# Query and key rows of a delta-rule layer left un-normalised, with their inverse lengths carried as factors per token

## The chip, the core and the metric

One core of a Trainium2 chip runs the whole program. The time is that of the device in microseconds (us), the median of three runs. The engines are TensorE (PE in the rows, its weight loads PEld), VectorE (DVE), ScalarE (ACT), GpSimd (POOL) and SyncE (SP), which here only issues DMAs.

## The reference, cut to what matters

The reference is two transformer blocks over 512 tokens of width 1024, in float32. The change lies in the second block, in its gated delta-rule branch:

```
qkv = silu(causal_conv(h @ w_qkv, conv_w))          # 4 taps, 3 x 1024 channels
q = l2_normalize(q) * DN_DK ** -0.5                  # per token and head, 8 heads of 128
k = l2_normalize(k)                                  # x * rsqrt(sum(x*x) + 1e-6)
beta = sigmoid(b);  g = -exp(a_log) * softplus(a + dt_bias)
o = chunk_gated_delta_rule(q, k, v, beta, g)
o = rms_norm(o, norm_g) * silu(z)
```

Within a chunk of 128 tokens the rule forms the matrix A[i,j] = beta_i * (k_i . k_j) * decay_ij below the diagonal, takes the inverse of (1 + A), applies it to beta * v and to beta * exp(g) * k, and updates a state of 128x128 per head. The rows of q enter the output only linearly, so a length left in them is a factor of the output row; the following root-mean-square norm has to know that factor because of its epsilon.

## The kernel before, in words

Each engine has its own instruction stream, written out in program order; semaphores couple the streams. Products go to eight PSUM banks in two rings of four: one ring is emptied by VectorE (`bank("dve")`, `take()` on VectorE), the other by ScalarE. An engine may run ahead of its partner by at most four banks.

The stage around the change, called the qkv stage here, comes after the sparse attention and before the delta rule. For two groups of four heads (g = 0, 1) and for the three parts q, k, v it makes four tiles of 128 channels by 512 tokens, 24 units in all. In a unit TensorE multiplies (eight matmuls of 128x512, each issued as two instructions, on the helper line 695), VectorE applies the four taps of the convolution out of the bank (L1884, L1889, then a one-element copy L1891 that frees the bank), and ScalarE applies silu in place (L2574).

Normalisation is interleaved. In each of the 16 units with part > 0, the tile made four units earlier (q while k is made, k while v is made) is normalised: VectorE squares it (L2075), TensorE multiplies it by a 128x128 matrix of ones so that each column holds the sum over the head's channels in all partitions (also L695), ScalarE takes the root (L2569) and signals with a small copy (L2571), VectorE takes the reciprocal over 128x512 (L2081) and multiplies the tile (L2082). VectorE's order in such a unit is: square, convolution, reciprocal, multiply; TensorE's order is: product of this unit, wait for the square, product with ones, product of the next unit.

After the 12 units of group 0, TensorE makes four row products for z (`z_rows`, L695 as well), emptied by ScalarE's silu (L2563). After group 1 it makes one, then `gains_along_rows` for both groups (16 instructions on L1173), which waits for VectorE's `gains_spread` (L2033). The stage thus holds 12 + 4 + 12 + 1 = 29 products of the same size and 16 products with ones.

Then come the chunks of the delta rule, `delta_step(g, ch, step)` with four chunks and 17 steps, the two groups alternating. On VectorE the odd steps below 14 update the inverse (L2131) and then do one part of the norm of the previous chunk's result (`result_norm`): part 1 is a reduction (L2054) and a multiply-add (L2055), part 2 a reciprocal of 128x4 (L2058). GpSimd masks and moves halves of the inverse (L2712, L2721). The inverse runs with five levels, on half-width matrices of 64 columns. Behind the last chunk, weight sums for the merge (L1765) wait for a weight transfer that SyncE starts after the last state update of the rule. `beg`, which is beta times exp(g), is made early, ahead of the index scores (L2005).

## Time and profile before

| | us |
|---|---|
| median of three runs (lowest, highest) | 2391.66 (2391.26, 2392.55) |
| the profiled execution, its own time | 2389.67 |
| its span, from the first to the last instruction | 2387.9 |
| TensorE busy | 2161.7 (91%) |
| VectorE busy | 1231.3 (52%) |
| ScalarE busy | 471.3 (20%) |
| qkv stage, from 1138.51 to 1361.66 of the span | 223.15 |

Rows give times from the start of the span. A timeline row has start, duration, engine, line, operation, output and input, and in brackets the idle time before it with what ended it. "x18" in a TensorE row is the number of merged instructions. The mean granted clock of TensorE is 0.955 of full speed in this execution.

### The profile page before, as it was taken

What the parts mean: (1) busy time and instruction counts of PE and PEld (TensorE: products, weight loads), DVE (VectorE), ACT (ScalarE), POOL (GpSimd) and SP (SyncE); (2) the same over time, 40 slices, a digit from 0 to 9 for tenths busy, and PEclk for the clock granted to TensorE, in tenths of its full rate; (3) what the DMA queues carried; (4) which work ended last, traced back from release to release, by engine and by line L of the source; (5) the groups of instructions that cost most, each with busy time, mean ns of one, the idle gap of its engine ahead of it and who ended that gap; (6) DMA issues with size and microseconds to landing.
All of it is one profiled execution on the core that took longest, in us unless ns stands there. A gap on an engine that the chain in (4) does not pass through costs nothing.

```text
span 2387.9 us, 23792 instructions
## 1 busy us (share of the span) xinstructions
PE 2161.7 (91%) x8806; PEld 1293.3 (54%) x8806; DVE 1231.3 (52%) x2129; ACT 471.3 (20%) x925; POOL 112.8 (5%) x143
## 2 busy tenths in 40 slices
PE   7998898999999999997999988899997799999873
PEld 3444344888888644434444466678864333333331
DVE  4684564666676522786575856677436321221113
ACT  1124441111000100125232433330001000000003
POOL 0000000000000000000000022210000010100000
PEclk9998898999999999899999999999998899999997
DMA  7126500522132212210111100021343799999994
GB/s 268 36 103 232 182 30 24 127 101 76 53 116 80 95 49 92 71 64 8 35 71 71 36 1 1 1 106 71 141 180 123 292 426 427 426 427 425 426 425 193
DMA packets 97289, 364.65 MB, mean 153 GB/s; under 512 B 10396, under 2 KB 19281, under 8 KB 84625
## 3 DMA queue, kind: packets, MB, share of 16 engines
q1 hardware_dynamic: 86337, 340.62, 36.9%
q0 software_dynamic: 8720, 20.89, 2.3%
q10 hardware_dynamic: 2112, 1.57, 0.2%
q8 instruction: 73, 1.20, 0.2%
q14 instruction: 47, 0.39, 0.0%
HBM read 357.00 MB, written 17.57 MB: 157 GB/s over the span
## 4 chain that ended last, share of the span: by engine, by line
PE 68%; DVE 16%; DMA 7%; ACT 4%; issue 4%; POOL 0%; SPq 0%; DVEq 0%; ACTq 0%; POOLq 0%
PE bank L695 45%; PE bank L1445 8%; PE bank L1440 5%; PE bank L760 2%; DVE mem L2081 2%; PE bank L1173 2%; PE bank L930 2%; DMA mem<-in_w_gate 2%; DMA mem<-in_w_down 2%; DMA mem<-in_w_up 2%; ACT mem L2405 1%; PE bank L805 1%; DVE mem L2022 1%; DVE mem L2021 1%; ACT L2569 1%
## 5 line engine op out<-in xcount | busy, mean ns | idle before, releaser
L695 PE MATMUL bank<-mem 128*128 128x256 f32 (+7 forms) x4688 | 1396.0, 459 | 39.8 <-ACT mem L2405 12.1
L695 PEld LDWEIGHTS bank<-mem 128*128 128x128 f32 (+1 forms) x4688 | 873.1, 193 | 512.1 <-issue 377.3
L1445 PE MATMUL bank<-mem 128*64 128x512 f32 x1248 | 283.5, 610 | 33.2 <-DMA mem<-in_w_up 13.4
L2405 ACT ACTIVATE mem<-bank 128x512 f32<-128x512 f32 (+6 forms) x262 | 133.9, 511 | 405.3 <-PE bank L695 159.6
L1445 PEld LDWEIGHTS bank<-mem 128*64 128x64 f32 x1248 | 93.5, 140 | 213.6 <-issue 201.2
L760 PE MATMUL bank<-mem 128*128 128x128 f32 (+1 forms) x692 | 118.8, 304 | 58.9 <-DVE mem L1679 24.2
L2341 DVE TENSOR_TENSOR mem<-mem,bank 128x512 f32<-128x512 f32 x19 | 13.1, 690 | 277.2 <-PE bank L1445 204.5
L760 PEld LDWEIGHTS bank<-mem 128*128 128x128 f32 (+1 forms) x692 | 85.1, 151 | 110.5 <-DVE mem L1679 37.2
L1440 PE MATMUL bank<-mem 128*128 128x512 f32 x288 | 128.9, 602 | 6.7 <-ACT mem L2665 4.1
L2518 ACT ACTIVATE mem<-bank 128x512 f32<-128x512 f32 (+1 forms) x50 | 29.1, 582 | 372.7 <-PE bank L695 371.0
L1440 PEld LDWEIGHTS bank<-mem 128*128 128x128 f32 x288 | 54.1, 191 | 76.6 <-issue 68.1
L2349 DVE TENSOR_TENSOR mem<-bank,mem 128x512 f32<-128x512 f32 x38 | 26.3, 693 | 106.6 <-PE bank L1445 73.9
L1173 PE MATMUL bank<-mem 128*128 128x128 f32 x512 | 69.0, 294 | 0.9 <-ACT mem L2405 0.8
L1173 PEld LDWEIGHTS bank<-mem 128*128 128x128 f32 x512 | 65.6, 208 | 3.5 <-ACT mem L2405 1.1
L2663 ACT ACTIVATE mem<-bank 128x512 f32<-128x512 f32 x19 | 11.4, 599 | 269.9 <-PE bank L1445 198.7
L2712 POOL TENSOR_TENSOR mem<-mem 128x256 f32<-128x256 f32 x40 | 36.9, 923 | 573.5 <-ACT mem L2405 561.2
L1765 DVE TENSOR_TENSOR mem<-mem 128x1024 f32<-128x1024 f32 (+2 forms) x25 | 29.1, 1163 | 56.1 <-PE bank L695 48.9
L2081 DVE RECIPROCAL mem<-mem 128x512 f32<-128x512 f32 x16 | 53.7, 3355 | 3.5 <-ACT mem L2571 3.5
L1889 DVE SCALAR_TENSOR_TENSOR mem<-bank,mem 128x511 f32<-128x511 f32 (+2 forms) x72 | 54.0, 750 | 2.6
L1884 DVE TENSOR_SCALAR mem<-bank,mem 128x512 f32<-128x512 f32 x24 | 18.0, 751 | 63.0 <-PE bank L695 62.5
L2665 ACT ACTIVATE mem<-bank 128x512 f32<-128x512 f32 x19 | 11.4, 599 | 172.0 <-PE bank L1461 172.0
L930 PE MATMUL bank<-mem 128*64 128x512 f32 (+7 forms) x128 | 41.7, 472 | 3.1 <-ACT mem L2405 3.1
(337 smaller groups left out, 1726.4 us busy)
## 6 DMA issues: line engine op xcount, KB each, us to landing
mem<-in_w_gate SPq DMA_DIRECT2D x37, 2048.0 KB, 25.2
mem<-in_w_up SPq DMA_DIRECT2D x37, 2048.0 KB, 24.4
mem<-in_w_down SPq DMA_DIRECT2D x36, 2048.0 KB, 26.0
mem<-in_w_in SPq DMA_DIRECT2D x18, 2048.0 KB, 7.7
mem<-in_w_ada SPq DMA_DIRECT2D x12, 2048.0 KB, 7.9
mem<-in_w_out SPq DMA_DIRECT2D x4, 2048.0 KB, 12.6
mem<-in_w_ple_gate SPq DMA_DIRECT2D x2, 2048.0 KB, 7.9
mem<-in_w_br_att SPq DMA_DIRECT2D x2, 2048.0 KB, 8.1
```

The costliest lines, as they stand in the source:

```text
L695: last = pe.matmul(o, l, r, start=(i == 0), stop=(i == len(pairs) - 1))
L760: last = pe.transpose(b[0:width, i * P:(i + 1) * P], s, ident)
L930: last = pe.matmul(o[:, k * P:SEQ], v_of(k, h), pT[:, h % nbuf, k, k * P:SEQ], start=(k == 0), stop=(k == NT - 1))
L1173: last = pe.matmul(b[:, h * P:(h + 1) * P], lhs(h), rhs(h), start=True, stop=True)
L1440: last_ = pe.matmul(o, lhs[:, k, :], ws[0][:, k, cols], start=(k == 0), stop=(k == kk - 1))
L1445: last_ = pe.matmul(o[here, :], lhs[:, k, here], w[:, k, cols], start=(k == 0), stop=(k == kk - 1))
L1765: V(tt(s1, feature_half(w, 0, 1), feature_half(w, 1, 1), ALU.add), w_summed)
L1889: V(stt(o, b[:, 0:SEQ - back], w_col(taps_ - 1 - back), o, ALU.mult, ALU.add), signal if back == taps_ - 1 else None)
L2081: V(dve.reciprocal(sq, sq))
L2405: C(act.activation(dst, src, ACT.Copy), act_free)
L2518: C(act.activation(dst[:, 0:cols], fast_bank(n, 3 * i)[:, 0:cols], ACT.Copy), fast_copied)
L2712: pool.tensor_tensor(B[f"L{lv % 2}"].rearrange("p h (a c) -> p h a c", a=half), level_order(B["AT"], lv)[:, :, half:2 * half, :], mask[:, ...
```

## The change

The query and key tiles stay as silu left them. ScalarE squares them instead of VectorE. TensorE sums the squares with four 128x128-by-one-column matmuls in place of one product with 512 columns, so that the sums stand per token in partitions, 4 columns per tile; VectorE adds epsilon and stores them in `lengths` (128 x 64 for q and k, 8 heads and 4 chunks). After the last unit one root on ScalarE and one reciprocal on VectorE serve all of them. The inverse length of k goes into beta: `beta_k` = beta/length scales v, and `beta` = beta/length squared scales A and, through `beg`, the keys. The inverse length of q times 128^-0.5 becomes a factor of the norm of the result (one multiply in part 1, one in part 2). The levels of the inverse are the same in both kernels; the diff holds no edit of them.

```diff
+        lengths = tiny(2 * NT * 8)
+        length_of = [lengths[:, j * NT * 8:(j + 1) * NT * 8].rearrange("p (a b) -> p a b", a=NT) for j in range(2)]
+        gain_of_q, gain_of_q2, beta_k = (tiny(NT * 8).rearrange("p (a b) -> p a b", a=NT) for _ in range(3))
...
 # TensorE, in each unit
                         if part:
-                            to_wait(to_pe)
-                            b = bank("act")
-                            full(product(b[:, :], [(const("ones"), flat(delta[0][("tmp", "decay")[i % 2]]))]), "act")
+                            to_wait(squares_ready)
+                            b = bank("dve")
+                            sq = flat(delta[0][("tmp", "decay")[i % 2]])
+                            for ch in range(NT):
+                                last = pe.matmul(b[:, ch:ch + 1], sq[:, ch * P:(ch + 1) * P], const("ones")[:, 0:1],
+                                                 start=True, stop=True)
+                            full(last, "dve")
+                            mark["squares", g, part, i] = done["dve"]
...
 # VectorE
-            V(tt(beg, beta, eg, ALU.mult))
...
                     V(dve.tensor_reduce(s, delta[g]["square"], AX.X, ALU.add))
+                    V(tt(s, s, gain_of_q2[:, ch, g * HG:(g + 1) * HG], ALU.mult))
                     V(ts(s, s, 1.0 / P, EPS, ALU.mult, ALU.add), square_summed[g])
                 if part == 2:
                     wait_next(square_rooted[g])
                     V(dve.reciprocal(s, s))
+                    V(tt(s, s, gain_of_q[:, ch, g * HG:(g + 1) * HG], ALU.mult))
...
-                        if part:
-                            before = S4["qkv"[part - 1]][:, g * HG + i, :]
-                            dve.wait_ge(silu_out, FT + 12 * g + 4 * (part - 1) + i + 1)
-                            sq = flat(delta[0][("tmp", "decay")[i % 2]])
-                            V(tt(sq, before, before, ALU.mult), to_pe)
                         m = part * 8 + g * 4 + i
                         conv(take(), S4[name][:, g * HG + i, :], CONV2,
                              lambda j: column("conv_w_2", j * 24 + m), None, silu_in)
                         if part:
-                            wait_next(from_act)
-                            V(dve.reciprocal(sq, sq))
-                            V(stt(before, before, DH ** -0.5 if part == 1 else 1.0, sq, ALU.mult, ALU.mult))
+                            V(ts(length_of[part - 1][:, :, g * HG + i], take()[:, 0:NT], EPS, None, ALU.add), dve_free)
+            V(dve.tensor_copy(stat8[:, 14:15], eps_col), lengths_summed)
             gains_spread(0, 0)
             gains_spread(1, 0)
+            wait_next(lengths_rooted)
+            V(dve.reciprocal(lengths, lengths))
+            V(ts(gain_of_q, length_of[0], DH ** -0.5, None, ALU.mult))
+            V(tt(gain_of_q2, gain_of_q, gain_of_q, ALU.mult))
+            V(tt(beta_k, beta, length_of[1], ALU.mult))
+            V(tt(beta, beta_k, length_of[1], ALU.mult))
+            V(tt(beg, beta, eg, ALU.mult))
...
-                    V(tt(B["v_b"], full_bank(), inner(beta[:, ch, gh], P), ALU.mult), dve_free)
+                    V(tt(B["v_b"], full_bank(), inner(beta_k[:, ch, gh], P), ALU.mult), dve_free)
...
 # ScalarE, in each unit
                         if part:
-                            C(act.activation(flat(delta[0][("tmp", "decay")[i % 2]]), take()[:, :], ACT.Sqrt,
-                                             bias=eps_col), act_free)
-                            C(act.activation(stat8[:, 15:16], eps_col, ACT.Copy), from_act)
+                            if i >= 2:
+                                act.wait_ge(dve_full, mark["squares", g, part, i - 2])
+                            elif part == 2:
+                                act.wait_ge(dve_full, mark["squares", g, 1, i + 2])
+                            C(act.activation(flat(delta[0][("tmp", "decay")[i % 2]]),
+                                             S4["qkv"[part - 1]][:, g * HG + i, :], ACT.Square), squares_ready)
                         wait_next(silu_in)
                         o = S4[name][:, g * HG + i, :]
                         C(act.activation(o, o, ACT.Silu), silu_out)
+                if g == 1:
+                    wait_next(lengths_summed)
+                    C(act.activation(lengths, lengths, ACT.Sqrt), lengths_rooted)
```

## Rows read from the trace of the kernel before

**Rows 1.** The first line of the page: the span.
```profile
span 2387.9 us, 23792 instructions
```
**Rows 2.** Chain of waits, 1120 to 1460: start, us, what.
```profile
1215.05 1.14 PE bank L695 x2
1216.25 1.28 ACT L2569
1218.57 3.37 DVE mem L2081
...
1231.83 63.06 PE bank L695 x146
```
**Rows 3.** Timeline of one unit with normalisation.
```profile
1215.05 8.01 PE L695 MATMUL bank<-mem 128*128 128x512 f32 x18 [0.39 <-DVE mem L2075]
...
1218.57 3.35 DVE L2081 RECIPROCAL mem<-mem 128x512 f32<-128x512 f32 x1 [0.25 <-ACT mem L2571]
...
1222.69 0.69 DVE L2075 TENSOR_TENSOR mem<-mem 128x512 f32<-128x512 f32 x1
...
1223.44 8.01 PE L695 MATMUL bank<-mem 128*128 128x512 f32 x18 [0.39 <-DVE mem L2075]
```
**Rows 4.** Windows, the qkv stage: us, busy and count by engine, granted clock.
```profile
1138.50:1361.60 223.10, 217.25 (x496) 92.59 (x496) 152.07 (x169) 74.17 (x93) 0.00 (x0) 1.00 0.16 57
```
**Rows 5.** Timeline, start of the stage and its end.
```profile
1138.51 42.40 PE L695 MATMUL bank<-mem 128*128 128x512 f32 x98 [0.85 <-DVE mem L2026]
...
1145.76 0.75 DVE L1884 TENSOR_SCALAR mem<-bank,mem 128x512 f32<-128x512 f32 x1 [7.31 <-PE bank L695]
...
1146.55 2.32 DVE L1889 SCALAR_TENSOR_TENSOR mem<-bank,mem 128x511 f32<-128x511 f32 x3
...
1152.64 0.75 DVE L1884 TENSOR_SCALAR mem<-bank,mem 128x512 f32<-128x512 f32 x1 [3.58 <-PE bank L695]
...
1361.66 2.05 PE L1173 MATMUL bank<-mem 128*128 128x128 f32 x16
```
**Rows 6.** Timeline of PE: other matmuls with few columns.
```profile
235.06 0.95 PE L819 MATMUL bank<-mem 128*128 128x1 f32 x8
...
969.85 0.95 PE L1135 MATMUL bank<-mem 128*128 128x8 f32 x8
```
**Rows 7.** Timeline of the delta rule around the norm of a result.
```profile
1444.25 0.86 POOL L2712 TENSOR_TENSOR mem<-mem 128x256 f32<-128x256 f32 x1
1444.57 0.56 DVE L2055 TENSOR_SCALAR mem<-mem 128x4 f32<-128x4 f32 x1
1445.16 0.42 DVE L2131 TENSOR_TENSOR mem<-mem,bank 128x256 f32<-128x256 f32 x1
...
1452.94 0.42 DVE L2131 TENSOR_TENSOR mem<-mem,bank 128x256 f32<-128x256 f32 x1 [2.31 <-PE bank L1284]
...
1454.76 0.17 DVE L2041 TENSOR_TENSOR mem<-mem 128x4 f32<-128x4 f32 x1
...
1587.91 0.17 DVE L2055 TENSOR_SCALAR mem<-mem 128x4 f32<-128x4 f32 x1
```
**Rows 8.** Timeline behind the last chunk.
```profile
1595.42 1.23 DVE L1765 TENSOR_TENSOR mem<-mem 128x1024 f32<-128x1024 f32 x1 [0.90 <-DMA mem<-in_w_br_att]
```
**Rows 9.** Timeline, small operations of VectorE ahead of the index scores.
```profile
973.01 0.19 DVE L2005 TENSOR_TENSOR mem<-mem 128x32 f32<-128x32 f32 x1 [1.70 <-ACT mem L2553]
```
**Rows 10.** Windows, a stretch of the delta rule with a lowered clock.
```profile
1410.00:1420.00 10.00, 7.13 (x50) 6.52 (x50) 2.22 (x4) 4.28 (x10) 0.00 (x0) 0.73 0.00 0
```
**Rows 11.** Timeline: the same product (eight instructions) at full and at lower clock.
```profile
1102.64 2.39 PE L930 MATMUL bank<-mem 128*128 128x512 f32 x8 [0.20 <-ACT mem L2405]
...
1133.05 4.60 PE L930 MATMUL bank<-mem 128*128 128x512 f32 x8 [0.84 <-ACT mem L2405]
```
**Rows 12.** Timeline of ACT: a square, then the table load of a root.
```profile
1791.02 1.15 ACT L2401 ACTIVATE mem<-mem 128x1024 f32<-128x1024 f32 x1
...
1792.28 1.28 ACT L2402 ACT_TABLE_LOAD   x1
```

More of the change, by code:

```diff
@@ L459, in build @@
         lower_moved = [sem(f"delta_lower_columns_moved{g}") for g in range(2)]
+        squares_ready, lengths_summed, lengths_rooted = (sem(f"qk_{n}") for n in ("squares_ready", "lengths_summed", "lengths_rooted"))
         square_summed, square_rooted, result_ready = ([sem(f"delta_{n}{g}") for g in range(2)]
```

## The prediction

> **What bounds the kernel now.** I read the chain of waits first, over the stage that the change touches. It alternates between two pictures. In the first five units and in the four z products it is TensorE alone, one product behind the other: the piece of 146 matmul instructions runs 63.06 us without a break [rows 2]. In a unit with normalisation it is a ring through three engines: two instructions of the product with ones on TensorE, a table load on ScalarE, the reciprocal of 3.37 us on VectorE [rows 2], then multiply, square, and TensorE again. The timeline says how long the ring is: TensorE starts the same group of 18 instructions at 1215.05 and at 1223.44, so a period is 8.39 us, and each time it has sat idle 0.39 us for VectorE's square [rows 3]. Without the ring a product takes 6.88 us, as the convolutions of two plain units start at 1145.76 and 1152.64 [rows 5]. So VectorE, at 8.39 us a unit, is the bound in this stretch, but TensorE is close behind it: the reader should see that an idle of 0.39 in 8.39 us is all that can be had there for taking VectorE away, plus what TensorE's own part of the normalisation shrinks. The window of the whole stage agrees: TensorE busy 217.25 of 223.10 us, at a granted clock of 1.00, VectorE 152.07 [rows 4].
>
> **The stage, new sum.** TensorE before: 29 products of 6.88 us are 199.5 us, 16 products with ones at two instructions of 0.43 us (6.88/16) are 13.8 us; together 213.3. The stage lasts 1361.66 - 1138.51 = 223.15 us [rows 5]. The other 9.8 us are idle time for VectorE and the refilling of the pipeline behind it: the first two instructions behind such a wait count 1.14 us in the chain instead of 0.86 [rows 2], and 0.39 + 0.28 = 0.67 in each of some 14 units is 9.4, which closes the account.
>
> After: four float32 matmuls of 128x128 by one column are eight instructions. The trace has the same shape elsewhere: eight on L819 in 0.95 us, and eight with 8 columns on L1135, again 0.95 us [rows 6]. The weight loads set this, not the columns. So the sums cost TensorE slightly more than before, 0.95 against 0.86 us, and a unit is 6.88 + 0.95 = 7.83 us if TensorE waits for nothing. Stage: 199.5 + 16 x 0.95 = 214.7 us, 8.4 us less than 223.15. Bounds: at 0.86 for a group the stage gains 10.0; if each group also pays the refill of 0.28 us seen behind a wait, 16 x 0.28 = 4.5 goes back and 3.9 is left. I take 8.4, since plain products follow each other at 6.88 us although each of them has a (satisfied) wait for a bank.
>
> The Trainium skill, TensorE: Matmul & The Clock Gate, section Back-to-back issue gap, gives about 81 ns for a sustained pair of weight load and matmul at 128 columns. By that the eight instructions would take 0.65 us and the stage would gain 13.2 us. The rows have 0.12 us each here (0.95/8), so the measurement speaks against that figure for float32 and I keep the row.
>
> Does TensorE wait? Take T as the end of a unit's product. VectorE convolves for 0.75 + 2.32 us and small change, until T + 3.3 [rows 5]. ScalarE then does silu and the square of the next unit, about 0.7 us each by the root's and square's size, until T + 4.8. TensorE wants that square at T + 7.83. There are 3 us of cover. A wait for the buffer two units back is long satisfied. VectorE now needs about 3.5 us a unit instead of 8.2: square, reciprocal and multiply are gone, 16 x (0.69 + 3.35 + 0.69) = 75.7 us of work, and all but the few us above were already beside TensorE. A small add of the sums (0.19 us, as L2005 [rows 9]) comes in their place, hidden. ScalarE loses 16 roots over 512 columns and both table loads per unit, 1.28 us each; they were in the ring, and go with it.
>
> **The end of the stage.** The new serial piece is: last sums, `lengths_summed`, root with a table load (1.28 + 0.25 us), reciprocal over 64 columns (3.35/512 x 64 = 0.42), five small operations of 0.19. From T of the last unit: VectorE at T + 3.9, the two `gains_spread` ahead of the wait, the root by T + 5.6, the rest by T + 7.1, two memsets (0.67 us) by T + 7.8. TensorE meanwhile has the sums and one z product in front of the gains: T + 7.83, and VectorE needs them 1 us later. So it is covered, by about 1 us; uncovered it would cost up to 1 us for every us it is longer. From the gains on, the order is as before. The load of silu's table for z moves to where ScalarE waits for the z product anyway. Cost 0, bounds 0 to 1.5.
>
> **The early edit.** L2005 leaves its place ahead of the index scores, where VectorE soon is the bound: -0.2 us [rows 9]; at the new place it is one of the five above. Bounds -0.2 to 0.
>
> **The delta rule.** 16 multiplies of 128x4 are added, two per result and group. The row nearest is L2041, the same operation and size, 0.17 us [rows 7], some 0.2 with its gap. Beside GpSimd's work a small operation is longer: L2055 takes 0.56 us and ends at 1445.13, when GpSimd's L2712, begun at 1444.25, ends; at 1587.91, with GpSimd idle, it takes 0.17 [rows 7]. The multiply stands ahead of L2055; it would meet GpSimd in its place, and L2055 would then be short, so I take the pair at 0.2 more, not 0.56. The six of part 1 in the chunks 1 to 3 stand in a stretch where VectorE has no gap and the other group's inverse update follows at once (L2131 at 1445.16): on the path, 6 x 0.2 = 1.2 us. The six of part 2 have 2.31 us of idle time behind them [rows 7]: 0. The four for the last chunk lie in front of the weight sums, which wait 0.90 us for a transfer [rows 8]; 4 x 0.2 = 0.8 is just covered: 0. Bounds: 0, where GpSimd or TensorE holds the path, to 16 x 0.56 = 9.0. I take 1.2.
>
> The Trainium skill, GPSIMD Engine Reference, section Key points, says that GpSimd shares its SBUF interfaces with VectorE and collides with instructions that have two SBUF inputs. The new multiplies are of that kind; by that rule alone each could be held as long as L2055 was. The trace agrees that there is such a hold (0.56 against 0.17).
>
> **Sum.** -8.4 - 0.2 + 1.2 = -7.4 us. All later work, routing and experts, starts from semaphores of this chain, so the gain passes on. The profiled execution: 2389.67 (span 2387.9 [rows 1] and 1.8 around it) becomes 2382.3. The median of the runs shown is 2391.66, 2.0 above it, so the predicted median is 2384.3, with 2381 to 2388 as this case's own range: the refill bound on one side, 0.86 us a group and a lucky clock on the other.
>
> **Rivals.**
> A. *Each group of one-column matmuls breaks the stream.* Its weight loads can't be fetched ahead across the wait, so 0.28 us [rows 2] comes 16 times: gain 7.4 - 4.5 = 2.9, median 2388.8. For it: the refill is seen behind each wait that held. Against: plain products wait too and lose nothing. Chance 0.10.
> B. *The bound moves to VectorE in the delta rule.* The multiplies take 0.56 us, 12 of them on the path: 6.7 instead of 1.2, gain 1.9, median 2389.8. For it: the 0.56 rows. Against: the hold ends with GpSimd's instruction, not per VectorE instruction. Chance 0.07.
> C. *Slower: TensorE's clock.* In the stage the granted clock was 1.00 [rows 4], full level, 2.4 GHz. Short one-column matmuls leave the array with little to do for 0.95 us in 7.83. In the delta rule, also made of small matmuls, the clock falls: 0.73 in a stretch of 10 us [rows 10]. The same eight instructions take 2.39 us at full and 4.60 at the lower level, 1.2 GHz [rows 11]. A product at the lower level costs 6.4 us more. From two such units on, beyond those in the trace now, the kernel is slower: 2384.3 + 12.7 = 2397. Against: today the array is idle for 0.39 us and refills for 0.28 in each unit, and holds 1.00. Chance 0.03.
> D. *Slower: ScalarE becomes the bound.* If square and silu need different tables, each unit has two loads as now: conv until T + 3.3, load, silu, load, square, T + 7.3: still in time for T + 7.83, with 0.5 us to spare, so the price by the rows is 0. A switch that took 1.4 us more than the load would end at T + 10, the period would be (10 + 7.83)/2 = 8.9 us, 0.5 more than now, and the kernel 16 x 0.5 - 0.2 + 1.2 = 9 us slower, 2401. The row of L2401 has a square in front of the root's load, not with one of its own [rows 12]. Chance 0.02. The Trainium skill, ScalarE: Activation LUTs, What ACT_TABLE_LOAD costs, does give a drain of 1.38 us beside each load of 1.28; the loads here are 1.28, and the root that followed one began within 0.02 us.
> E. *More is gained:* sums at 0.86 or less, the additions of the delta rule off the path, or fewer stretches at the lower clock because everything after the stage falls at other moments. 10.2 and more, median 2381 or less. Chance 0.08.
> F. *It does not do what it says.* The levels of the inverse are not edited; nothing is to be had from them, and I count nothing. The rest could only show less by a path I take for serial being covered elsewhere (a transfer behind the stage): gain 0 to 4, about 2390. Chance 0.05.
>
> **How the numbers follow.** The forecast holds 0.65. About 0.2% (4.8 us) is what a measurement of this kernel tells from no change. Faster by more: 0.61 of the forecast's 0.65 and E's 0.08, minus a little for the share of clock luck: 0.70 in round numbers. Within 0.2%: A, B, F and the weak end of the forecast, 0.25. Slower: C and D, 0.05. The range 2380 to 2389.5 takes in A and most of E, and leaves out B, C, D and part of F.
>
> **What would show each step.** In the profile after: starts of the convolutions (L1884's successor) 7.83 us apart in units of part 1 and 2, TensorE without waits on VectorE or ScalarE in the stage, and some 214.7 us from 1138.3 to the gains; eight one-column matmuls in 0.95 us; one table load for the root in the stage, not 32; the distance from the gains to the last chunk's end longer by about 1.2 us. Wrong it would be with a period near 8.1 (A), with multiplies of 0.56 us each (B), with a granted clock under 1.00 in the stage (C), or with TensorE waiting for ScalarE's square (D).

## The result

The kernel after the change takes 2379.49 us (median of 6 executions, 2373.22 to 2382.63), the kernel before, timed beside it, 2392.11 us (6, 2390.81 to 2396.48). The ratio is 0.9941, with a 95% interval of 0.9924 to 0.9957: 14.1 us faster, and with that interval between 10.3 and 18.2 us (the two medians are 12.6 us apart). Forecast were 2384.3 and -7.4 us. The direction was right. The gain was larger than the forecast: the median lies 0.5 us below the range of 2380 to 2389.5, and 1.5 us below the narrower one, from 2381, that the forecast's sum also gives.

The two profiled executions show less of it: 2380.66 us after against 2389.67 before, 9.0 us. One execution against another does not settle a few microseconds in this kernel, as will be seen. The first lines of the page of the kernel after; the second line answers to "busy" in the table of before:

```profile
span 2378.8 us, 23910 instructions
...
PE 2160.2 (91%) x8902; PEld 1304.1 (55%) x8902; DVE 1162.9 (49%) x2119; ACT 428.5 (18%) x880; POOL 112.1 (5%) x143
```

The unit that [rows 3] showed before looks like this after (timeline; start, us, engine, line, operation, tiles and shapes, count, idle time before and who ended it; weight loads left out):

```profile
1182.99 0.95 PE L1198 MATMUL bank<-mem 128*128 128x1 f32 x8
...
1183.26 0.75 DVE L1893 TENSOR_SCALAR mem<-bank,mem 128x512 f32<-128x512 f32 x1 [4.27 <-PE bank L699]
...
1183.80 7.13 PE L699 MATMUL bank<-mem 128*128 128x512 f32 x16
1184.05 2.32 DVE L1898 SCALAR_TENSOR_TENSOR mem<-bank,mem 128x511 f32<-128x511 f32 x3
...
1186.46 0.63 ACT L2588 ACTIVATE mem<-mem 128x512 f32<-128x512 f32 x1 [6.48 <-DVE mem L1898]
1186.59 0.17 DVE L2085 TENSOR_SCALAR mem<-bank 128x4 f32<-128x4 f32 x1
...
1187.13 0.63 ACT L2584 ACTIVATE mem<-mem 128x512 f32<-128x512 f32 x1
...
1190.76 0.95 PE L1198 MATMUL bank<-mem 128*128 128x1 f32 x8
...
1191.04 0.75 DVE L1893 TENSOR_SCALAR mem<-bank,mem 128x512 f32<-128x512 f32 x1 [4.28 <-PE bank L699]
```

No row of TensorE has a bracket any more: it waits for nothing. VectorE has taken over the waiting, 4.27 us in each unit. The period is 1190.76 - 1182.99 = 7.77 us, against 8.39 in [rows 3]. The square ends at 1187.76, 3.0 us before TensorE wants it. The stage as a whole (windows: length, then busy us and count of PE, PEld, DVE, ACT, POOL, then the granted clock of TensorE, DMA share, GB/s), beside [rows 4]:

```profile
1140.70:1354.60 213.90, 213.89 (x592) 102.11 (x593) 80.94 (x145) 30.46 (x47) 0.00 (x0) 1.00 0.17 59
```

TensorE is busy for all of 213.90 us where it was for 217.25 of 223.10; VectorE fell from 152.07 to 80.94 us, ScalarE from 74.17 to 30.46. The clock is 1.00 as before.

**Where the difference of the profiles lies.** I cut every profiled execution at the same five places: first product of the stage, first gains matmul, last matmul of the gains' line L1173 (L1177 after), first weight sum of the merge (VectorE, L1765, L1774 after), first silu of the experts (ScalarE, L2663, L2680 after). Lengths in us, worked out from the starts in the timelines:

```
                    to stage   stage   delta rule   end of it   merge, routing   rest
before              1138.51   223.15     223.70       10.07        280.50       511.95
after               1140.71   213.92     224.29       10.00        277.47       512.44
difference            +2.20    -9.23      +0.59       -0.07         -3.03        +0.49
```

Two sections gained. The stage is the one forecast at -8.4. The other, -3.0 us between the delta rule and the experts, is in no step of the forecast, and no instruction was edited there.

### The profile page after: what moved, and what is told of

Its sections match the earlier page's. It is cut to its first block, busy times and chain, and to the rows that moved or that the text cites. A ratio compares the mean times of both kernels' runs of the same rounds, so it can differ in the third digit from the quotient of the medians.

```text
span 2378.8 us, 23910 instructions
## 1 busy us (share of the span) xinstructions
PE 2160.2 (91%) x8902; PEld 1304.1 (55%) x8902; DVE 1162.9 (49%) x2119; ACT 428.5 (18%) x880; POOL 112.1 (5%) x143
## 4 chain that ended last, share of the span: by engine, by line
PE 73%; DVE 13%; DMA 7%; issue 4%; ACT 3%; POOL 0%; SPq 0%; DVEq 0%; ACTq 0%; POOLq 0%
PE bank L699 49%; PE bank L1454 8%; PE bank L1449 5%; PE bank L764 2%; PE bank L1177 2%; DMA mem<-in_w_gate 2%; PE bank L934 2%; DMA mem<-in_w_down 2%; DMA mem<-in_w_up 2%; ACT mem L2416 1%; PE bank L809 1%; DVE mem L2030 1%; DVE mem L2029 1%; DMA mem<-in_w_in 1%; PE bank L1430 1%
## 5 line engine op out<-in xcount | busy, mean ns | idle before, releaser
L699 PE MATMUL bank<-mem 128*128 128x256 f32 (+6 forms) x4656 | 1380.4, 458 | 33.4 <-ACT mem L2416 13.5
L1177 PE MATMUL bank<-mem 128*128 128x128 f32 x512 | 69.1, 294 | 0.8 <-ACT mem L2416 0.8
L1177 PEld LDWEIGHTS bank<-mem 128*128 128x128 f32 x512 | 65.8, 209 | 3.1 <-ACT mem L2416 1.1
L2680 ACT ACTIVATE mem<-bank 128x512 f32<-128x512 f32 x19 | 11.4, 598 | 278.1 <-PE bank L1454 206.8
L1774 DVE TENSOR_TENSOR mem<-mem 128x1024 f32<-128x1024 f32 (+2 forms) x25 | 29.1, 1163 | 55.1 <-PE bank L699 47.8
L2588 ACT ACTIVATE mem<-mem 128x512 f32<-128x512 f32 x24 | 15.2, 631 | 147.6 <-DVE mem L1898 147.6
```

What stands on the lines that cost most here:

```text
L699: last = pe.matmul(o, l, r, start=(i == 0), stop=(i == len(pairs) - 1))
L1177: last = pe.matmul(b[:, h * P:(h + 1) * P], lhs(h), rhs(h), start=True, stop=True)
L1774: V(tt(s1, feature_half(w, 0, 1), feature_half(w, 1, 1), ALU.add), w_summed)
```

## The experiments

Two theories stood at the outset. The first, the forecast's: the stage gains because TensorE no longer waits in the ring of three engines; the order of the work does it, not the amount. Its rivals are the removed 75.7 us of VectorE's work and the removed table loads. The second theory came from the table above: something behind the stage gains as well, by the clock, by moment, or by the lengths per token. "Ratio" is always to the kernel before on the same chip, with its 95% interval.

**1. The kernel after, again** (no edit).

> The changed kernel once more, to size the scatter. Theory 1 (the prediction missed by its size, and the rest is the clock): the qkv stage lasts 214.0 us again, and the time against the kernel before lies between -8 and -14 us; the spread of single times, some 9 us, goes with the mean granted clock, which had 0.958 at the lowest of 2373.22 and 0.950 to 0.953 at the others. Rival (something systematic of 3 to 5 us behind the stage is gained too): the time differs from before by -12 to -13 us again, at any clock, and the delta rule up to the merge is shorter by the same amount in this profile as in the first one.

Measured: 2378.92 us (5 executions) against 2394.57 (16), ratio 0.9941 (0.9928 to 0.9955). The sections of its profile: stage 213.92, delta rule 224.38, merge and routing 277.64. The result and the gain behind the stage repeat. That gain is not where the rival expected it: the delta rule is no shorter, the section behind it is.

**2. The square alone to ScalarE**, the rest as before: root, reciprocal and multiply of every unit stay.

```diff
@@ the kernel before, VectorE @@
-                            dve.wait_ge(silu_out, FT + 12 * g + 4 * (part - 1) + i + 1)
-                            V(tt(sq, before, before, ALU.mult), to_pe)
@@ ScalarE @@
+                            if u >= 2:
+                                act.wait_ge(tile_normalised, u - 1)
+                            C(act.activation(flat(delta[0][("tmp", "decay")[i % 2]]),
+                                             S4["qkv"[part - 1]][:, g * HG + i, :], ACT.Square), squares_ready)
```

> The kernel before with one edit: ScalarE makes the squares, right behind the silu of the unit ahead; root, reciprocal and multiply over 128x512 stay. Theory 1 (TensorE stood still because VectorE's square sat behind the reciprocal and multiply of the unit ahead, not because VectorE had too much to do): TensorE finds the square ready, a unit takes 6.88 + 0.86 = 7.74 us instead of 8.39, the stage 214 us plus about 1 at its end for the last reciprocal and multiply, so 8 to 9 us less than 223.15, the same as the whole change got. Rival (the reciprocal keeps VectorE the bound): VectorE's share of a unit only falls by the square, 0.72 us, and waits for the root in addition, so a unit takes 8.0 us or more and at most 5 us are gained.

Measured: 2386.77 us (11), ratio 0.9971 (0.9962 to 0.9980), 7 us faster. VectorE's timeline in this kernel:

```profile
1204.58 0.75 DVE L1885 TENSOR_SCALAR mem<-bank,mem 128x512 f32<-128x512 f32 x1 [0.32 <-PE bank L696]
...
1207.91 3.35 DVE L2080 RECIPROCAL mem<-mem 128x512 f32<-128x512 f32 x1
1211.30 0.69 DVE L2081 SCALAR_TENSOR_TENSOR mem<-mem 128x512 f32<-128x512 f32 x1
1212.32 0.75 DVE L1885 TENSOR_SCALAR mem<-bank,mem 128x512 f32<-128x512 f32 x1 [0.32 <-PE bank L696]
```

The reader should see two things. The reciprocal of 3.35 us and the multiply are still there, and yet VectorE waits for TensorE (0.32 us), so TensorE is the bound: the period is 7.74 us. And the stage, from 1146.59 to 1360.39, is 213.80 us. So all of the stage's gain comes from taking the square, 0.69 us in each unit, out of the place where TensorE waited behind reciprocal and multiply for it. The lengths per token are not needed for it. At the end the gains wait 0.31 us for VectorE, no more. But the section of merge and routing is 280.97 us here: what the full change gains there is missing, and so is about half of its total. The time fell by less than the stage did, 7 against 9.35 us; in this profile the delta rule lasts 226.07 us (223.70 before), with 27.3 us of it at a lowered clock against 20.5.

**3. The reciprocal back into the kernel after**, as added work whose result nobody reads (nothing is left out).

```diff
@@ the kernel after, VectorE, per unit @@
+                            dve.wait_ge(silu_out, FT + 12 * g + 4 * (part - 1) + i + 1)
+                            V(dve.reciprocal(flat(delta[0]["A"]), S4["qkv"[part - 1]][:, g * HG + i, :]))
```

> The changed kernel with a reciprocal over 128x512 put back on VectorE in each of the 16 units, of a silu'ed tile into a buffer that nobody reads: 53.7 us of work that nothing waits for. Theory 1 (the gain was the order, not the work): VectorE then has 3.5 + 3.4 = 6.9 us in a unit of 7.78, the stage stays at 214 us, or 1 to 3 us longer at its end, where the last reciprocal lies in front of the lengths' root. Rival (the reciprocal itself was the gain): the stage goes back toward 223 us.

Measured: one time, 2380.98 us (the kernel before beside it: 2391.26). The timeline:

```profile
1206.92 0.75 DVE L1893 TENSOR_SCALAR mem<-bank,mem 128x512 f32<-128x512 f32 x1 [0.89 <-PE bank L699]
...
1210.46 3.35 DVE L2087 RECIPROCAL mem<-mem 128x512 f32<-128x512 f32 x1
...
1214.70 0.75 DVE L1893 TENSOR_SCALAR mem<-bank,mem 128x512 f32<-128x512 f32 x1 [0.89 <-PE bank L699]
```

16 x 3.35 = 53.6 us of work are back on VectorE, the period is still 7.78, and the stage 214.01 us. They fill idle time (4.27 us becomes 0.89). That rival is refuted: these 53.6 of the removed 75.7 us were worth 0.1 us. The multiplies and the squares, the other 22 us, were not put back here; in experiment 2 the multiplies stayed, and the stage gained all the same.

**4. Two table loads per unit back into the kernel after** (a root of one element ahead of the square; nothing is left out). This is rival D of the forecast, built.

```diff
@@ the kernel after, ScalarE, per unit @@
+                            C(act.activation(stat8[:, 15:16], eps_col, ACT.Sqrt))
                             C(act.activation(flat(delta[0][("tmp", "decay")[i % 2]]),
                                              S4["qkv"[part - 1]][:, g * HG + i, :], ACT.Square), squares_ready)
```

> The changed kernel with a root over one element on ScalarE ahead of each square, so that both table loads are back in each of the 16 units, in the chain from a unit's silu to the next unit's square. By the prediction's sum the square is then ready 7.3 us behind the end of the unit ahead, against 7.8 when TensorE asks for it: theory 1 says stage 214 us, no change. Rival D of the prediction (a switch costs more than its load, some 1.4 us for each): squares come late, TensorE waits for ScalarE, units of 8.9 us, the stage 16 us longer.

Measured: one time, 2383.34 us; stage 213.92.

```profile
1202.83 0.75 DVE L1893 TENSOR_SCALAR mem<-bank,mem 128x512 f32<-128x512 f32 x1 [4.28 <-PE bank L699]
...
1206.01 1.28 ACT L2589 ACT_TABLE_LOAD   x1 [3.67 <-DVE mem L1898]
...
1207.95 1.28 ACT L2584 ACT_TABLE_LOAD   x1
...
1209.48 0.63 ACT L2585 ACTIVATE mem<-mem 128x512 f32<-128x512 f32 x1
...
1210.33 0.95 PE L1198 MATMUL bank<-mem 128*128 128x1 f32 x8
```

The square ends at 1210.11, and TensorE takes up the sums at 1210.33, with no wait. Counted from the start of the unit's convolution (1202.83), the square is ready at 7.3 us, the number that the forecast had, and TensorE wants it at 7.5. Even with both loads, and the added root of 0.20 us, the price in the stage is 0, but only 0.2 us of cover are left. D is refuted.

**5. q's length as an epsilon.** The normalised result doesn't change when q is scaled, if the epsilon is scaled with it. So the 16 added multiplies of the delta rule can go.

```diff
@@ the kernel after, VectorE, norm of a result @@
-                    V(tt(s, s, gain_of_q2[:, ch, g * HG:(g + 1) * HG], ALU.mult))
-                    V(ts(s, s, 1.0 / P, EPS, ALU.mult, ALU.add), square_summed[g])
+                    V(stt(s, s, 1.0 / P, length_of[0][:, ch, g * HG:(g + 1) * HG], ALU.mult, ALU.add),
+                      square_summed[g])
...
-                    V(tt(s, s, gain_of_q[:, ch, g * HG:(g + 1) * HG], ALU.mult))
```

> The changed kernel with the 16 small multiplies of the result's norm taken out: since r/sqrt(L*128) over its root mean square is r/sqrt(mean(r*r) + eps*L*128), q's squared length L is stored as eps*128*L and added where eps was, in one instruction that was there before. Theory 1: the multiplies cost 0.2 us each where VectorE has no gap, six of them, so 1.2 us less than the changed kernel, perhaps 0 within what can be measured; the trace shows L2055's successor at its old place. Rival (GpSimd's hold, 0.56 us for each): 5 us less or more. Rival 2: they are hidden, 0 us.

Measured: 2377.26 us (6), ratio 0.9936 (0.9923 to 0.9950), beside 0.9941 (0.9928 to 0.9955) of the kernel after, timed with it. 1.7 us less is the direction and size forecast for the multiplies (1.2), but the intervals overlap almost wholly: not told apart. The delta rule is 224.94 us in its profile and 224.29, 224.38 and 224.39 in three of the kernel after, with one more stretch of 3.4 us at a lowered clock, so the profile doesn't show the gain either.

**6. q's sums out of the stage**, on top of the last. In the stage TensorE is the bound, in the delta rule it waits. The eight groups for q are computed there, a chunk behind.

```diff
@@ TensorE, stage and delta rule @@
-                        if part:
+                        if part == 2:
                             to_wait(squares_ready)
...
+            def q_sums(g, ch):
+
+                to_wait(q_squared[g])
+                b = bank("dve")
+                for h in range(HG):
+                    last = pe.matmul(b[:, h:h + 1], delta[g]["square"][:, h, :], const("ones")[:, 0:1],
+                                     start=True, stop=True)
+                full(last, "dve")
@@ ScalarE, delta rule, step 12 @@
+                        C(act.activation(B["square"], S4["q"][:, g * HG:(g + 1) * HG, ch * P:(ch + 1) * P], ACT.Square),
+                          q_squared[g])
```

> As the kernel with q's length in the epsilon, and the squares and sums of q moved out of the qkv stage into the delta rule: ScalarE squares a chunk of four heads at step 12, TensorE sums it at step 1 of the next chunk, ahead of its wait for VectorE. Theory 1 (TensorE bounds the qkv stage and has idle time in the delta rule): the stage loses 8 groups of 0.90 us, 7.2 us, and the delta rule gets at most 2 to 3 back, so 4 to 6 us less than the kernel with the epsilon. Rival (the delta rule is a chain in which anything put in counts): 8 groups of 0.9 us, 8 reads of 0.2 and 8 squares of 0.65 us there cost 7 us or more, no gain or a loss of up to 5 us.

Measured: 2370.26 us (4, 2367.93 to 2373.32), ratio 0.9900 (0.9885 to 0.9916). This is the fastest version: 24 us under the kernel before, 8.7 under the kernel after timed with it, with intervals that don't touch, and 7.0 under experiment 5, on which it is built. That is more than the 4 to 6 us expected. From its timeline, a stretch of the delta rule:

```profile
1411.37 0.95 PE L1337 MATMUL bank<-mem 128*128 128x1 f32 x8
...
1412.72 0.95 PE L1337 MATMUL bank<-mem 128*128 128x1 f32 x8
...
1413.66 0.16 DVE L2071 TENSOR_SCALAR mem<-bank 128x4 f32<-128x4 f32 x1
```

The stage is 206.77 us (start 1139.62, gains 1346.40), 7.15 less, which is 8 x 0.9. The delta rule is 225.41, 0.5 more than in experiment 5. The same instructions, 0.95 us a group, cost nearly nothing where TensorE waits anyway.

**7. The place of `beg`.** The profile of before has a stretch of 6.8 us with the clock lowered just ahead of the stage, and the profiles of the kernel after have none; the multiply `beg` was moved away there. Three runs ask whether that place makes the stretch, and whether it is worth time: `beg` moved alone in the kernel before; in the kernel after, a multiply of the same size put back at the old place (nothing left out); the kernel before again for one more profile.

```diff
@@ beg_late_alone: the kernel before, VectorE @@
-            V(tt(beg, beta, eg, ALU.mult))
...
             gains_spread(1, 0)
+            V(tt(beg, beta, eg, ALU.mult))
@@ beg_early_too: the kernel after, VectorE @@
+            V(tt(beg, beta, eg, ALU.mult))
```

> The kernel before with one edit: the multiply for `beg` is made behind `gains_spread` and no longer ahead of the index scores. Open is the rest of the measured 12 to 15 us beyond 9.2 us in the qkv stage. In the profiles with `beg` early (before, square_moved_only) TensorE is at the lower clock for 6.8 us at the end of the sparse attention, and for 3.4 us at the start of the merge; in the four profiles with `beg` late it is at neither. Theory 1 (0.2 us less ahead of the attention shifts it against the clock's changes, so that the stretch at the attention's end is missed): the profile has no lowered clock in the 20 us before the qkv stage, the time is 2 to 3 us below that of before, though the edit itself saves 0.2 us. The merge's stretch hangs on the length of the stage and may stay. Rival (chance): the stretch is there, and the time is that of before within 1 us.

> The changed kernel with the multiply for `beg` made at its old place as well as at the new one, 0.2 us more of work. Theory 1: the stretch of lowered clock at the end of the sparse attention is back (about 2.4 us), and the time is 2 to 4 us above that of the changed kernel. Rival (chance): the profile has no lowered clock there and the time is that of the changed kernel within 1 us.

> The kernel before, unedited, for a second profile. The stage lasts 223.15 us. If the rest of the gain is systematic, the two stretches at the lower clock, at the end of the sparse attention and at the start of the merge, are there again, and from the merge's weight sums to the first expert's silu it takes 280 to 281 us; if they are chance, either may be missing.

Measured: `beg` late alone 2394.08 us (12), ratio 1.0009 (0.9996 to 1.0021); `beg` early too 2380.43 (5), ratio 0.9956 (0.9943 to 0.9969); the kernel before, one time, 2396.49, with 223.17 us in the stage and 283.50 from the merge to the experts, outside the 280 to 281 expected. Windows of the end of attention, first the kernel before (this profile), then with `beg` late alone:

```profile
1138.00:1146.00 8.00, 6.24 (x14) 3.50 (x15) 0.70 (x2) 0.77 (x2) 0.00 (x0) 0.57 0.00 0
```

```profile
1122.00:1136.00 14.00, 10.03 (x41) 5.80 (x42) 6.33 (x21) 5.82 (x16) 0.00 (x0) 1.00 0.00 1
```

The stretch (clock 0.57 in 8 us) is in both profiles of before and in that of `beg` early too, and absent where `beg` is late (1.00). But the time doesn't follow: 1.0009 contains no gain. The theory that the place of `beg` gains time by the clock falls. It also isn't a rule: experiment 4 has `beg` late and has the stretch.

These profiles show what the kernel's own scatter is made of. The part ahead of the stage lasts 1138.51 and 1145.46 us in two executions of the same kernel before:

```profile
0.00:1145.50 1145.50, 1057.30 (x4001) 678.79 (x4001) 667.35 (x1313) 228.75 (x494) 6.53 (x13) 0.95 0.28 94
```

The work is the same (VectorE 667.60 us in one, 667.35 in the other), and TensorE is busy for 1049.36 in one and 1057.30 in the other, since it spends 102 and 120 us at a lowered clock. In all thirteen profiles taken this part lies between 1135.4 and 1146.6, in no order with the edits. It goes with the time at the lowered clock: 95.6 us of that in the two profiles of 1136.4 and 1136.5, 122.9 us in that of 1146.6, and the other ten lie within 2.5 us of a straight line between these.

**8. The stage made long again.** Does merge and routing gain because it comes at another moment, or because of the edits? The kernel after gets 22 product instructions of 0.43 us more at the end of the stage, 9.5 us, in a bank that is overwritten (nothing left out); and the kernel after itself has one more profile beside it.

```diff
@@ the kernel after, TensorE, ahead of the last z product @@
+                if g == 1:
+                    b = banks[4 + done["act"] % 4]
+                    pe.wait_ge(act_free, done["act"] - 3)
+                    product(b[:, :], [(hT[:, k, 0:P], w_z[:, k, :]) for k in range(KD)])
+                    product(b[:, :], [(hT[:, k, 0:P], w_z[:, k, :]) for k in range(3)])
                 z_rows(0)
```

> The changed kernel with 11 more matmuls of 128x512 (22 instructions of 0.43 us, 9.5 us, their result overwritten by the next product) ahead of group 1's first z product: the qkv stage is then as long as before, 223.4 us, and every edit of the change stays. It tells what the gain behind the stage hangs on: from the merge's weight sums to the first expert, four profiles without the lengths per token take 280.5 to 283.5 us, seven with them 277.5 to 279.8. Theory 1 (when the merge comes, against the clock's changes): 280.5 us or more, a stretch of lowered clock at the start of the merge, and a time at or above that of the kernel before. Rival (something the edits take away there, as the shorter transfer, 7.7 us against 8.5 to 8.8): 277.5 to 279 us, and a time 3 to 5 us below that of before.

> The changed kernel beside it, for one more profile on the same chip: stage 213.9 us, and from the merge's weight sums to the first expert 277 to 280 us; a value of 280.5 us or more would say that the difference between the two kernels there is scatter.

Measured: lengthened, 2388.16 us (9), ratio 0.9979 (0.9968 to 0.9991); the kernel after, one time, 2378.34. The stage is 223.38 us again, as in before (223.15). Merge and routing now, in all profiles (us):

```
without lengths per token              with lengths per token
before               280.50            after              277.47
before, again        283.50            after, again       277.64
beg late alone       280.72            after, last        277.75
square moved only    280.97            reciprocal back    277.95
                                       epsilon            278.09
                                       q's sums moved     277.62
                                       stage lengthened   278.77
                                       tables back        278.91
                                       beg early too      279.75
```

The two columns don't overlap, the stage's length makes no difference to the column, and the lengthened kernel still beats the one before by 5 us. So this gain goes with the edits and not with the moment. The start of the section in three kernels, before, after, and lengthened (SyncE's issue of the weight transfer, and the TensorE group that waits for it):

```profile
1586.50 0.37 SPq L2804 DMA_DIRECT2D mem<-in_w_br_att  x1
...
1595.02 8.86 PE L695 MATMUL bank<-mem 128*128 128x256 f32 x32 [2.51 <-DMA mem<-in_w_br_att]
```

```profile
1580.06 0.37 SPq L2821 DMA_DIRECT2D mem<-in_w_br_att  x1
...
1587.77 7.17 PE L699 MATMUL bank<-mem 128*128 128x256 f32 x32 [1.70 <-DMA mem<-in_w_br_att]
```

```profile
1587.30 0.37 SPq L2826 DMA_DIRECT2D mem<-in_w_br_att  x1
...
1595.07 7.17 PE L699 MATMUL bank<-mem 128*128 128x256 f32 x32 [1.76 <-DMA mem<-in_w_br_att]
```

From the issue to the first matmul pass 8.5, 7.7 and 7.8 us, and TensorE is idle 2.51, 1.70 and 1.76 of them. Then the same 32 instructions take 8.86 us in the first and 7.17 in the others. The windows say why (10 us of before, of after, of the lengthened kernel; the clock stands third from the end):

```profile
1595.00:1605.00 10.00, 9.98 (x42) 8.55 (x43) 9.34 (x8) 0.58 (x1) 0.00 (x0) 0.83 0.98 361
```

```profile
1588.00:1598.00 10.00, 10.00 (x51) 8.82 (x51) 9.69 (x10) 1.94 (x4) 0.00 (x0) 1.00 1.04 380
```

```profile
1595.00:1605.00 10.00, 9.93 (x50) 8.78 (x51) 9.69 (x10) 2.14 (x5) 0.00 (x0) 1.00 1.05 386
```

In before the granted clock came down for 3.4 us just behind the wait of 2.51 us; in the other two, with waits of 1.70 and 1.76, it did not. That is 1.7 of the 3.0 us between the profiles of before and after. Another 0.75 us is the transfer's earlier arrival: TensorE restarts 0.40 us ahead of the first weight sum in the one and 1.15 us ahead of it in the other. The remaining 0.6 us lies in small differences along the section and has no single row. Over all profiles the wait is 2.51 to 2.75 us without the lengths per token and 1.70 to 1.98 with them, except where q's sums were moved: there TensorE has other work until the weights are in and does not wait. The stretch is in all of the first kind and, of the second, in `beg` early too, with a wait of 1.91, 8.86 us for the 32 instructions and, fitting to that, the longest section of its column. So the longer wait and the lower clock go together, but the length of this wait alone does not decide it.

Why the transfer arrives sooner after its issue stands in the DMA queues (packets, MB, share of the 16 engines' time) between its issue and TensorE's restart, before and after:

```profile
q1 hardware_dynamic: 1320, 2.67, 88.4%
q8 instruction: 1, 0.02, 0.9%
```

```profile
q1 hardware_dynamic: 1183, 2.39, 84.9%
```

In before one packet of 16 KB, of the kind that the profile calls "instruction", starts 1.07 us behind the issue and takes 1.28 us, where the transfer's own packets of 2 KB take about 0.09 each. The transfer lands in 16 parts. In after all of them are there by 7.66 us behind the issue; in before 15 are there by 7.89, and the last one comes at 8.48. All profiles divide this way. The four without the lengths per token have the packet, 0.95 to 1.26 us behind the issue, and one late part at 8.48 to 8.72 with the other 15 by 7.93. The nine with them have no such packet before the landing, and all parts are there by 7.95; the next packet of the kind comes 11.6 us behind the issue in the lengthened kernel and 16.9 us or later in the others. So the longer wait goes with this packet in all thirteen profiles, and the edits, which change the instruction streams, moved it out of the transfer. By its name it loads code. That the lengths per token as a method have nothing to do with it is argued from this and not shown: no run moved the packet alone.

## Why the prediction was right in direction and short in size

- **What bounded the stage** held. The ring of three engines, with TensorE just behind it, was the right reading: TensorE is busy all through the stage after, and the square 3 us early, as forecast. Experiment 2 sharpened it: what mattered was the square's place behind reciprocal and multiply.
- **The stage's size** was a little off: 213.92 against 214.7 forecast, a gain of 9.2 against 8.4. The term that was mis-sized is the 0.95 us per group of eight one-column matmuls. That is how long a group is; what it adds to the stream is 7.774 - 6.88 = 0.894 us (7.774 is the mean period in the profile after), because its end overlaps the next product's start (the product starts 0.81 us after the group in the rows of the result). 16 x 0.056 = 0.9 us. The bound of 10.0 us for groups of 0.86 us was added up wrongly: 223.15 - 213.3 is 9.85. The Trainium skill, TensorE: Matmul & The Clock Gate, Back-to-back issue gap, gives about 81 ns for a pair at 128 columns; an estimate from it was a gain of 13.2. The runs show 0.11 us for each of these float32 instructions (0.894/8) and a gain of 9.2.
- **The end of the stage** held, 0: the fifth small operation ends at 1354.50, the gains start at 1354.63, and VectorE itself then waits for them:

```profile
1352.46 0.26 ACT L2591 ACTIVATE mem<-mem 128x64 f32<-128x64 f32 x1
...
1352.82 0.56 DVE L2090 RECIPROCAL mem<-mem 128x64 f32<-128x64 f32 x1 [1.08 <-ACT mem L2591]
...
1354.31 0.19 DVE L2095 TENSOR_TENSOR mem<-mem 128x32 f32<-128x32 f32 x1
1354.62 0.67 DVE L2097 MEMSET mem<- 128x256 f32 x2
1354.63 1.95 PE L1177 MATMUL bank<-mem 128*128 128x128 f32 x16
...
1355.79 0.69 DVE L2045 TENSOR_TENSOR mem<-mem,bank 128x512 f32<-128x512 f32 x1 [0.50 <-PE bank L1177]
```

- **The delta rule** held, in mechanism for sure. The forecast was that the new multiply takes GpSimd's hold in place of the small operation behind it, and that the pair costs 0.2 us more. It does:

```profile
1438.30 0.87 POOL L2729 TENSOR_TENSOR mem<-mem 128x256 f32<-128x256 f32 x1
...
1438.61 0.57 DVE L2063 TENSOR_TENSOR mem<-mem 128x4 f32<-128x4 f32 x1
...
1439.21 0.17 DVE L2064 TENSOR_SCALAR mem<-mem 128x4 f32<-128x4 f32 x1
1439.42 0.42 DVE L2142 TENSOR_TENSOR mem<-mem,bank 128x256 f32<-128x256 f32 x1
```

  The multiply is held for 0.57 us until GpSimd's instruction ends at 1439.17, then the addition takes 0.17; before it was 0.56 for the addition alone [rows 7]. The section is longer by 0.6 us in the pair of profiles, 1.2 were forecast; the two profiles of the kernel before are themselves 1.0 us apart there (223.70 and 222.67), so its size is not measured. Rival B (6.7 us) is refuted by the rows. The sign that the forecast gave for it, multiplies of 0.56 us, is seen and was badly chosen: what counts is the pair. The Trainium skill, GPSIMD Engine Reference, Key points, has the collision of the two engines for instructions with two SBUF inputs; these rows add that a held instruction frees the next one, and [rows 7] that L2055, with one tensor input, was held as well.
- **Rival A** (0.28 us of refill per group) is refuted by the period of 7.77, **rival C** by the clock of 1.00 in the stage, **rival D** by experiment 4. **Rival F** fails in its half about something covered elsewhere: more came than was counted, not less.
- **The step that failed** is the last one of the sum: "All later work, routing and experts, starts from semaphores of this chain, so the gain passes on". It put everything behind the delta rule at 0, and the runs show -3.2 us there, between the delta rule and the experts, as the difference of the means of the two kinds of profile. The stage's gain does pass on (the lengthened kernel takes 9.5 us more in the stage, and the ratios 0.9979 and 0.9941 are 9.1 us apart), but other time came with it. In the pair of profiles it is 1.7 us for 32 matmuls at full instead of lowered clock, 0.75 for a transfer that lands sooner, and 0.6 without a row.
- **Rival E** is where the median came out (2381 or less), at a chance of 0.08. It named "fewer stretches at the lower clock because everything after the stage falls at other moments", priced at no row. There was one stretch less, at the merge. The second half of the reason was wrong, since making the stage long again did not bring the time back. Its other reasons, shorter groups and a cheaper delta rule, gave 0.9 us and nothing that could be measured. The forecast has no term for the packet in the transfer: that this part of the gain came was luck.
- **The account.** -9.2 for the stage, -3.2 for merge and routing (the means of the two columns of experiment 8, 281.4 and 278.2), +0.6 for the delta rule: -11.8 us. That is inside the interval of the timed runs, -10.3 to -18.2; their middle, -14.1, is 2.3 us further, the difference of the medians, -12.6, only 0.8. The lengthened kernel is off by as much: -5.0 measured, -2.6 by the same terms without the stage. Whether these 2 us are more than scatter is open; no section of a profile shows them.

## What to carry to other kernels

When two engines are nearly level in a ring, ask which single instruction the other waits for and what stands ahead of it in its queue: moving that one square per unit gave the whole 9 us of the stage, while 54 us of work on the same engine were worth 0.1. Then move small work that can't be removed from the stage where its engine is the bound into one where it waits (8 groups of 0.9 us, 7 us gained). And when a forecast says "everything behind is only shifted", look at the waits for transfers, the packets that fall into them and the lowered-clock stretches just behind the change, and give their shift a price in both directions. A gain of this kind is not owed to the idea of the change, and another kernel need not get it.

## What the runs showed of the hardware that was not expected

- One packet of kind "instruction", 16 KB and 1.0 to 1.5 us long, inside a weight transfer of 2 MB went with one of its 16 parts landing at 8.5 to 8.7 us instead of by 7.95, in 4 of 4 profiles with the packet and in none of 9 without.
- A wait for a transfer that is 0.8 us longer went with another 1.7 us behind it: 32 matmuls of 128x256 took 8.86 us, with the clock lowered, behind a wait of 2.51 us, and 7.17 behind one of 1.70. In one profile they took 8.86 behind a wait of 1.91.
- The same program lasts between 1138 and 1146 us up to the stage, because TensorE spends 102 to 120 us of it at a lowered clock. A gain of 7 us cannot be read from one pair of executions; the whole kernel's single times scatter by 9 to 12 us.
- Two table loads of 1.28 us in each unit of 7.8 us, with the activations behind them starting within 0.02 us, cost nothing here.
